# Seven products instead of eight in twelve more projections, and half of the weight sums of the second block made by adding DMA transfers

## What is computed

```python
# first block
z = rmsnorm(x) @ w_in                 # hq, hf, hi(=hv), hg, c_q, c_kv, k_rope, gate_a, gate_b
o_a = hgrn2_mixer(hq, hf, hi, hg)     # gated linear recurrence over the tokens
o_b = mla_mixer(c_q, c_kv, k_rope)    # causal attention
y = sigmoid(gate_a) * (o_a @ w_branch_hgrn) + sigmoid(gate_b) * (o_b @ w_branch_mla)
x = x + y @ w_out
x = x + hierarchical_moe(rmsnorm(x))  # 64 experts, their weights are 400 MB
# second block: z = rmsnorm(x) @ w_in_2, three attentions with gates, an output projection
```

## Time and profile before

| | us |
|---|---|
| median of 3 runs | 1601.92 (1600.97 to 1602.46) |
| the profiled execution | 1599.81 |
| its span | 1598.0 |
| TensorE busy | 1270.6 (80%) |
| VectorE busy | 450.5 (28%) |
| ScalarE busy | 198.6 (12%) |
| GpSimd busy | 0.5 |

### The profile page before, as it was taken

How to read it: one execution, slowest core, us unless ns; L and a number is a source line. 1 busy time by engine, 2 the same in 40 slices (tenths; PEclk the granted TensorE clock), 3 DMA queues, 4 the chain that set the end, 5 groups by cost and what they waited for, 6 DMA issues and landing times.

```text
span 1598.0 us, 19255 instructions
## 1 busy us (share of the span) xinstructions
PE 1270.6 (80%) x8526; PEld 776.0 (49%) x8526; DVE 450.5 (28%) x788; ACT 198.6 (12%) x402; POOL 0.5 (0%) x5
## 2 busy tenths in 40 slices
PE   9999999999746856656656665565676999989998
PEld 8656887864313412212212221221221578989985
DVE  3254343232100100100101010010010477698522
ACT  2002023120000000000000000000000211135411
POOL 0000000000000000000000000000000000000000
PEclk9999999999988877877877877887788999999999
DMA  9342256389999999999999999999999654424340
GB/s 387 110 181 107 87 182 256 161 359 402 442 427 437 431 433 430 437 435 433 438 431 436 430 436 431 438 428 440 431 436 426 262 200 159 159 106 164 114 158 27
DMA packets 20558, 506.90 MB, mean 317 GB/s; under 512 B 4240, under 2 KB 4368, under 8 KB 6544
## 3 DMA queue, kind: packets, MB, share of 16 engines
q1 hardware_dynamic: 20208, 505.70, 75.6%
q10 hardware_dynamic: 288, 0.26, 0.0%
HBM read 504.91 MB, written 1.05 MB: 317 GB/s over the span
## 4 chain that ended last, share of the span: by engine, by line
PE 56%; DMA 39%; DVE 3%; issue 1%; ACT 0%; SPq 0%; DVEq 0%; ACTq 0%
DMA ring<-in_experts 37%; PE psP L1218 23%; PE psP L655 9%; PE psP L1270 6%; PE psP L703 4%; PE psP L1268 4%; DMA arena<-in_experts 2%; PE psA L718 2%; PE psP L1371 1%; PE psB L1588 1%; DVE arena L1869 1%; PE psB L1204 1%; PE psA L634 1%; DVE ring L1869 0%; PE psP L1317 0%
## 5 line engine op out<-in xcount | busy, mean ns | idle before, releaser
L655 PE MATMUL psP<-arena 128*32 128x512 f32 x1024 | 145.3, 718 | 130.8 <-DMA arena<-in_experts 130.6
L655 PE MATMUL psP<-ring,arena 128*32 128x512 f32 x1024 | 146.0, 721 | 129.8 <-DMA ring<-in_experts 129.8
L1869 DVE TENSOR_TENSOR X<-X,psA 128x512 f32<-128x512 f32 x66 | 45.3, 688 | 695.5 <-PE psA L718 681.4
L1218 PE MATMUL psP<-arena,ring 128*128 128x256 f32 x896 | 196.1, 379 | 0.0
L1218 PEld LDWEIGHTS psP<-arena,ring 128*128 128x128 f32 x896 | 169.2, 190 | 23.0 <-issue 0.3
L655 PEld LDWEIGHTS psP<-ring,arena 128*32 128x32 f32 x1024 | 37.2, 129 | 235.2 <-issue 231.5
L655 PEld LDWEIGHTS psP<-arena 128*32 128x32 f32 x1024 | 35.1, 129 | 235.4 <-DMA arena<-in_experts 120.2
L1218 PE MATMUL psP<-ring,arena 128*128 128x512 f32 (+2 forms) x368 | 141.9, 543 | 0.0
L1218 PEld LDWEIGHTS psP<-ring,arena 128*128 128x128 f32 x368 | 65.9, 190 | 67.5 <-issue 67.0
L703 PE MATMUL psP<-arena 128*32 128x512 f32 x512 | 66.8, 681 | 26.9 <-DMA arena<-in_experts 25.6
L703 PE MATMUL psP<-ring,arena 128*32 128x512 f32 x512 | 65.9, 667 | 25.8 <-DMA ring<-in_experts 24.5
(11 more groups left out here) (339 smaller groups left out, 1161.9 us busy)
## 6 DMA issues: line engine op xcount, KB each, us to landing
arena<-in_experts SPq DMA_DIRECT2D x7, 4096.0 KB, 21.3
ring<-in_experts SPq DMA_DIRECT2D x7, 4096.0 KB, 22.7
ring<-in_u_gl SPq DMA_DIRECT2D x6, 2048.0 KB, 8.2
ring<-in_u_hq SPq DMA_DIRECT2D x2, 2048.0 KB, 23.5
ring<-in_u_hv SPq DMA_DIRECT2D x2, 2048.0 KB, 12.1
ring<-in_u_hg SPq DMA_DIRECT2D x2, 2048.0 KB, 9.2
ring<-in_u_ga SPq DMA_DIRECT2D x2, 2048.0 KB, 8.6
ring<-in_u_gb SPq DMA_DIRECT2D x2, 2048.0 KB, 8.9
```

The costliest lines, as they stand in the source:

```text
L655: mm = pe.matmul(z[j * CAP:(j + 1) * CAP, :], x[:, 4 * half + k, j * CAP:(j + 1) * CAP], held[c % 4][:, k // 2, j, (k % 2) * 512:(k % 2 + ...
L1218: mm = pe.matmul(dsts[o], lhs_of(o, k), rhs_of(o, k), start=(k == 0), stop=(k == kc - 1))
L1869: return dve.tensor_tensor(o, a, b, op)
```

## The change

Twelve projections of the first block (`FIRST`) and `dq` of the second now go by seven products. `hf0 hf1 cl ch hg1 ga1`, the small ones and `wo0 wo1` stay plain. In the first block VectorE makes all sums, with new buffers; t4 is made by a new step `late`, once product 1 is done. Results that ScalarE read from PSUM before (`hq hg ga gb`) are now merged by VectorE into SBUF first, and ScalarE applies its function there in place. `wa` and `wb` are merged and then multiplied with their gates.

In the second block, for the fifteen units from `dv` on (`BY_DMA`), t1 and t3 are no longer made on VectorE. SP loads one quarter of the weights (512 KB) into the t1 buffer, GpSimd issues a transfer that adds a second quarter from HBM onto it, and another that adds a quarter from HBM onto the one in the ring (t3). VectorE keeps t2 and t4. `sums("xg")` moves from behind `normal 6` to right behind the merge of `mg`. The host lays out the units of `FAST` by quarters. The signs of some sums change, so that t1 and t3 are pure additions. The scaling of X, two operations of 128x1024 from one SBUF buffer to another, moves on VectorE from the step `root_row mid` to the end of `halves mid`.

```diff
+FIRST = ["hq0", "hq1", "hv0", "hv1", "hg0", "ga0", "gb0", "gb1", "wa0", "wa1", "wb0", "wb1"]
+FAST = FIRST + ["dq", "dv", "dk", "mv", "mq", "dg", "mk", "mg", "xq", "xg", "gl0", "gl1", "gl2", "gl3", "gl4", "gl5"]
+BY_DMA = FAST[len(FIRST) + 1:]
@@ plan
-    proj("hf0", "hf1", "hq0", "hq1", "hv0")
+    proj("hf0", "hf1")
+    p.append(("halves", "x", ""))
+    sums("hq0")
+    sums("hq1")
+    late("hq0")
+    proj("hq0")
+    sums("hv0")
+    late("hq1")
+    proj("hq1")
+    sums("hv1")
+    late("hv0")
+    proj("hv0")
     p.append(("level", 0, "AB"))
+    before = {"cl": "hg0", "hg1": "ga0", "ga1": "gb0", "gb0": "gb1"}
...
+        if fill[n - 1] in before:
+            sums(before[fill[n - 1]])
+        if fill[n - 1] in FIRST:
+            late(fill[n - 1])
         proj(fill[n - 1])
...
     p.append(("norm", "mid", "AB"))
+    p.append(("sums", ("dq", 0), ""))
     p.append(("stats", "mid", ""))
+    p.append(("sums", ("dq", 1), ""))
...
     proj("mg")
+    sums("xg")
     p.append(("head", ("xq", 16), ""))
...
     p.append(("normal", 6, ""))
-    sums("xg")
     proj("xq")
@@ SP, second block, ahead of the load of unit n
+                if n and UNITS_2[n - 1][0] in BY_DMA:
+                    arg = UNITS_2[n - 1][0]
+                    q = BY_DMA.index(arg)
+                    if q:
+                        wait_full(sp, ("proj", FAST[FAST.index(arg) - 2]))
+                    else:
+                        wait_full(sp, ("proj", "iq"))
+                    sp.dma_start(sums_of(arg)[0], quarter_in(arg, 0, 0)).then_inc(t1_in[q % 2], 16)
                 load(UNITS_2, n)
@@ GpSimd
+            for q, arg in enumerate(BY_DMA):
+                pool.wait_ge(t1_in[q % 2], 16 * (q // 2 + 1))
+                pool.dma_start(sums_of(arg)[0], quarter_in(arg, 0, 1), accum_op=ALU.add).then_inc(t1_made[q % 2], 16)
+                wait_unit(pool, arg)
+                pool.dma_start(quarter_of(arg, 0, 1), quarter_in(arg, 1, 1), accum_op=ALU.add).then_inc(t3_made[q % 2], 16)
@@ VectorE
                 else:
-                    dve.wait_ge(summed, n_summed[0] - 1)
-                    n = told(tt(t2, w[:, 4:KC, high], t1, ALU.subtract))
-                    dve.wait_ge(summed, n)
-                    told(tt(t4, w[:, 4:KC, low], t2, ALU.subtract))
+                    if arg in BY_DMA:
+                        q = BY_DMA.index(arg)
+                        dve.wait_ge(t1_made[q % 2], 16 * (q // 2 + 1))
+                    else:
+                        dve.wait_ge(summed, SUMMED[arg] - 1)
+                    tt(t2, as_sums(b22, t2), as_sums(t1, t2), ALU.add).then_inc(summed, 1)
+                    if arg not in FIRST:
+                        dve.wait_ge(summed, SUMMED[arg])
+                        tt(t4, b21, t2, ALU.add).then_inc(summed, 1)
+            def add_late(arg):
+                t1, t2, t4 = sums_of(arg)
+                dve.wait_ge(made, 2 * FAST.index(arg) + 1)
+                dve.wait_ge(summed, SUMMED[arg])
+                tt(as_sums(t4, t2), as_sums(quarter_of(arg, 1, 0), t2), t2, ALU.add).then_inc(summed, 1)
```

More of the change, by code:

```diff
@@ L186, in sums, with late @@
         p.extend([("sums", (name, 0), ""), ("sums", (name, 1), "")])
+    def late(name):
+        p.append(("late", name, ""))
     def turn(g, following, *names, then=(), after=None):
@@ L201, in turn @@
             p.append(("sums", (after, 1), ""))
+        if g == 0:
+            sums("wa1")
+            late("wa0")
         if g == 9:
@@ L232, in plan @@
     p.append(("hg_outT", 0, "AB"))
+    p.append(("halves", "oa", ""))
+    sums("wa0")
     proj("kn0", "kn1")
@@ L459, in build @@
         relu_s = area(8, 2, 512, off=1024)
-        score = sb("score", [P, 384])
-        dmask = sb("dmask", [P, 384])
         sg = {"mg": area(10, 4, S), "dg": area(10, 4, S, off=1024), "xg": area(11, 4, S)}
         gl = [area(0, KC, S), area(1, KC, S), area(2, KC, S)]
-        h_sums = spare[:, 512:2560].rearrange("p (a k n) -> p a k n", a=4, k=4)
+        four_sums = lambda ap: ap.rearrange("p (a k n) -> p a k n", a=4, k=4)
+        h_sums = {"x": four_sums(spare[:, 0:2048]), "oa": area(4, 4, 4, P), "ob": area(6, 4, 4, P),
+                  "mid": four_sums(spare[:, 512:2560])}
         ring_free = ring[:, SLOTS_2, :]
+        in_fours = lambda ap: ap.rearrange("p (k n) -> p k n", k=4)
+        w_spare = [in_fours(spare[:, 2048 + 1024 * i:3072 + 1024 * i]) for i in range(2)]
+        w_10, w_7, w_8 = ([area(a, 4, 256, off=1024 * i) for i in range(2)] for a in (10, 7, 8))
+        w_apart = [area(8, 4, 256, off=1024), C[:, :, 0:512].rearrange("p t (k n) -> p t k n", k=2)]
+        first_sums = {"hq0": w_spare, "hq1": w_10, "hv0": w_spare, "hv1": w_10, "hg0": w_spare, "ga0": w_10,
+                      "gb0": w_spare, "gb1": w_apart,
+                      "wa0": w_7, "wa1": w_8, "wb0": w_7, "wb1": w_8}
         w_sums = [[x.rearrange("p (k n) -> p k n", k=4) for x in t] for t in
@@ L1919, in blocks @@
                 return ap.rearrange("p h (n b) -> p (h n) b", b=2 * b)
-            n_summed = [0]
+            last_used = {"hv0": "hq0", "hv1": "hq1", "hg0": "hv0", "ga0": "hv1", "gb0": "hg0", "wb0": "wa0", "wb1": "wa1"}
+            last_used |= {n: FAST[FAST.index(n) - 2] for n in FAST[len(FIRST) + 2:]}
             def add_up(arg, part):
-                w, (t1, t2, t4) = unit_ap(arg), sums_of(arg)
-                low, high = slice(0, 256), slice(256, 512)
-                def told(i):
-                    n_summed[0] += 1
-                    i.then_inc(summed, 1)
-                    return n_summed[0]
+                (b11, b12), (b21, b22) = ([quarter_of(arg, kh, nh) for nh in range(2)] for kh in range(2))
+                t1, t2, t4 = sums_of(arg)
```

198 lines of the change are left out of this document (145 added, 53 removed).

## The result

The changed kernel takes **1625.26 us** (median of 4, 1617.19 to 1626.15); the kernel before, run beside it, 1601.45 (1600.88 to 1602.46). The ratio is 1.0137, 95% interval 1.0104 to 1.0170: slower, where the prediction said 1592 us and faster, with a range of 1583 to 1606. The profiled execution took 1625.0 us, its span is 1623.2.

The account below looks back on a forecast made before the run. TensorE was taken to bound both blocks, DMA the experts' stage. Gains of 12.0 (first block), 1.7 (`dq`) and 1.3 (later turns), less 2.2, 1.8 and 1.1, gave 9.9 us: 1592 us, range 1583 to 1606.

Parts of the forecast that it names:

- t3 has 6 us of slack ahead of product 7: nothing: Second block, from the later turns' term: making t3 by an adding transfer costs nothing, having 6 us of slack.
- D: Second block: time the adding transfer for t1 takes, forecast 7.4 us, between 3.8 and 13.0; each us beyond costs 6.5.
- The limit: Second block: D may be 6.9 us before anything is lost; each further us costs half a us per projection.
- First block 12.0: First block: twelve projections by seven products save 16.5 us, VectorE's stops lose 4.5, so it ends 12.0 us earlier.
- `dq` 1.7: Second block, projection `dq` by seven products: 1.7 us gained, its sums just covered ahead of `stats mid`.
- `dv` 2.2: Second block, projection `dv`: its quarter stands behind its own 2048 KB load, so 2.2 us are lost.
- `dk` to `xq`, 1.8: Second block, seven projections: D of 7.4 against 6.9, half the excess lost in each, 1.8 us in all.
- `xg` 1.1 lost: Second block: t2 and t4 of `xg` delay `soft 6` by 5.8 us, 4.75 of sums go: 1.1 lost.
- The later turns, 1.3 gained: Second block after `xg`: VectorE is 2.3 us lighter in each turn and three short stops go, 1.3 us gained.
- The slow one: Rival, second block: adding transfers slow, D above 8.9, kernel slower than before, 1615 us at D = 11; chance 0.21.
- The cheap one: Rival, second block: adding transfers cheap, D at most 5.7, 15.1 us gained, 1587 us; chance 0.24.
- The first block was not worse: Rival: VectorE's in-order queue costs the first block twice the forecast, or its gain is partly lost, 1596.5 us; chance 0.10.

Follow-up runs that it names:

- `xg` back: The changed kernel with the sums of xg moved back behind normal 6: 1627.78 us, ratio 1.0166.
- t3 only: The changed kernel, but only t3 is made by an adding transfer, VectorE makes t1, t2 and t4: 1580.74 us, ratio 0.9883.
- room 1024: The changed kernel with 1024 instead of 512 bytes per partition for GpSimd's transfer descriptors, `small` made smaller: 1609.14 us, ratio 1.0056.
- without adding transfers: The changed kernel with VectorE making all four sums in the second block: 1582.57 us; with the xg sums back behind normal 6: 1589.09 us.
- Early and alone, t1: The changed kernel, only t1 by adding transfer (t3 on VectorE), its plain quarter issued after product 5 of the projection two before: 1592.90 us, ratio 0.9952.
- t1 only: The changed kernel, but only t1 is made by an adding transfer, VectorE makes t2, t4 and t3: 1606.58 us, ratio 1.0039.
- room 1024 and the early quarter: The changed kernel with 1024 descriptor bytes and t1's plain quarter issued after product 5 of the projection two before: 1597.47 us, ratio 0.9984.
- room 1024 and the load after t1: The changed kernel with 1024 descriptor bytes, SP issuing the next unit's 2048 KB load only once t1 is made: 1605.34 us, ratio 1.0034.

## Why the prediction was wrong

**The step that failed** is half a sentence: "t3 has 6 us of slack ahead of product 7: nothing". It is true of TensorE, which in the changed kernel's trace never waited for t3 (with `xg` back it did twice, 1.48 and 0.57 us), and the run with t3 only shows it free. But t3 is issued on the same GpSimd queue as the next t1, and with room for one transfer it holds that t1 back until it has landed. What the prediction called D, from the landing of the quarter to the landing of t1, was 8.28 + 5.84 = 14.1 us at `mv`, above the 13.0 that stood as the upper row. That bound was made of bandwidth alone: it had the load beside the transfer in it, and not the transfer ahead of it. The price: 14 to 16 us go with 1024 bytes of room. The front of this document shows the very rows, t3 between two t1 on GpSimd; I read their order and priced each transfer by itself.

**Mis-sized: D.** Even with room for two it is 8.5 and not 7.4, and by the prediction's own slope of 6.5 us that alone is 7. The limit was 6.1 and not 6.9. The half us per projection beyond it came out at `mv` and `dg` and 0.5 too small at `mg`. And the forecast's own range, 1585 to 1598, didn't follow from its D: by the same slope 5.7 and 8.9 give 1587 and 1602.

**Missing: the clock.** The prices took no account of what TensorE does after a stop. The windows view of the changed kernel, behind the stops at `dv` and at `mq` (the columns as above; the clock is the third from the end):

```profile
1285.86:1291.07 5.21, 5.21 (x16) 4.29 (x17) 5.11 (x16) 0.00 (x0) 0.00 (x0) 0.67 1.03 341
1291.20:1296.00 4.80, 4.80 (x24) 4.23 (x23) 2.98 (x9) 0.38 (x1) 0.88 (x1) 1.00 0.40 147
...
1339.44:1343.10 3.66, 3.66 (x17) 3.25 (x18) 1.27 (x4) 0.00 (x0) 0.00 (x0) 1.00 1.07 359
```

After 2.38 us of standing still the granted clock over the first projection rows is 0.67, a mean between the levels of 1.2 and 2.4 GHz, and 5 us later it is back at 1.00. After 1.51 us at `mq` it stays at 1.00. I had the like of it before my eyes in the earlier trace rows, 5.44 us behind a stop of 4.10. Taken in windows of 2 us over the second block (TensorE's busy time times what the clock lacks to 1.00), the lower clock comes to 12.4 us in the changed kernel, all of it at the stops from `dv` to `probsT 6`, and to 1.7 in the kernel before, at `xg`: 10.7 of the 36.7 us.

**By terms.** First block 12.0: measured 11.3 (11.5 in the traces), the stops in the places named and 1.1 us smaller in sum. So the products by themselves gave 14.9 us and not 16.5; in that part the nearly right sum is luck, and the runs don't say where the 1.6 are. `dq` 1.7: 1.2 up to `xg`, nothing at the end. `dv` 2.2: the stop is 2.38, and 4.1 with the clock. `dk` to `xq`, 1.8: 18.6 us of stops and some 9 of clock. `xg` 1.1 lost: about 2 lost, since the stop at `probsT 6` that was to stay at 4.10 is 5.11, with another of 1.84 where TensorE waits for `soft 6` (stops and slower matmuls: 4.10 + 1.6 in the earlier trace rows, 1.84 + 5.11 + 0.9 here); without adding transfers the move alone gains 6.5. The later turns, 1.3 gained: four stops of 0.32, 0.52, 0.84 and 1.57 us are there instead of the three of 1.3 in sum, 1.9 lost.

**The rivals.** The slow one was the right side, its break-even of D = 8.9 was passed, but by a queue and not by slow transfers, so that its "for" (GpSimd has never issued a transfer here) was better than its mechanism. The cheap one is refuted by D at `mv` in both runs, 14.1 and 8.5. The first block was not worse than laid out: 3.4 us of stops, not 9. Of the two rules of the Trainium skill weighed there: that an adding transfer, which reads two sources, runs at half the rate of a copy ("Collectives: The Full Stack", Part 3, said there of ReduceScatter) isn't borne out here: 8.52 us against 7.04 at `mv`, 1.2 to 1.7 times over all units. The trap "DVE blocks DMA" ("SBUF — State Buffer") shows little: the scaling of X ran from 1273.18 to 1274.59, GpSimd's issue for `dv` began at 1274.04, 0.30 us after the quarter had landed, and took 1.00 us instead of 0.88. With room 1024 an issue at `mv`, with no such operation beside it, began 0.34 us after its quarter, so the 0.30 is no delay and 0.12 us are left, against the 1.4 that I had worked out.

**Open.** How many adding transfers 1024 bytes hold is not shown, nor why two copies fit in 512. That the build's 512 bytes are what held GpSimd is shown by changing them alone (with `small` made smaller for it); how it comes to wait is not. One of the four runs of the changed kernel took 1617.19, 8 us less than the others, and I have no trace of it. Early and alone, t1 took 1592.90, 12.2 us more than t3 only, most of it at `dv` and `xg`; whether it would catch up with these two in another order was not tried.

## What to carry to other kernels

Before work goes from an engine to a queue that has carried nothing so far, write down everything that this queue will issue, in its order, and ask of each entry what it holds back, also where its own consumer has slack; and find out how many transfers may be under way on it at once. Move to it only what has slack, one transfer per unit: t3 alone cost nothing against VectorE's sums, t1 alone 24 us. And price a stop of TensorE of some 2 us or more with the slower matmuls that can stand behind it, here 1.5 us on top in most cases.

## What the runs showed of the hardware that I had not expected

- GpSimd issued a second adding transfer of 512 KB only when the first had landed, with 512 bytes per partition for descriptors; with 1024 the two issues were 0.54 us apart, and two plain copies were 0.56 apart with 512.
- An adding transfer of 512 KB took 5.7 to 5.8 us when it was issued after the load had landed (a plain one of SP's, issued just ahead of a load, mostly 3.6 to 4.3). Beside a load it took 8.1 to 9.0 in the run with t1 only and up to 12.3 as t3 in the changed kernel. The longest, with room 1024 and the early quarter, took 14.1.
- Behind TensorE's stops the next matmuls were slower, the granted clock 0.67 over 5.2 us at `dv`. In the second block of these runs it was so behind all the stops of 2.81 to 5.11 us and behind none up to 1.87; in between both were seen (with room 1024 and the load after t1, 3.69 us as at full clock behind a stop of 2.38, and 5.44 instead of 3.81 behind one of 2.22).
